# First scale vector of a two-layer encoder kernel: matrix columns moved past one column of silu(c), sums left as a row

## The chip, the cores and the metric

The kernel runs on one core of one Trainium2 chip. The metric is the device time of one execution in microseconds (us). PE is TensorE, DVE is VectorE, ACT is ScalarE, POOL is GpSimd, and SP is SyncE, which here only issues transfers.

## What is computed

A hybrid encoder trunk of two layers on x of 256 rows and 2048 columns. Each sub-layer is preceded by an RMS norm, modulated with a shift and a scale that are projected from the vector c:

```python
def _modulate(x, shift, scale):
    return _rmsnorm(x) * (1 + scale[:, None, :]) + shift[:, None, :]

mod_all = jnp.einsum('bd,lde->lbe', jax.nn.silu(c), ada_w) + ada_b[:, None, :]
for i in range(DEPTH):
    shift1, scale1, gate1, shift2, scale2, gate2 = jnp.split(mod_all[i], 6, axis=-1)
    h = _modulate(x, shift1, scale1)
    ...
    # layer 0: time mixing (three D x D projections of token-shifted h first), layer 1: sparse attention
    x = x + gate1[:, None, :] * y
    h = _modulate(x, shift2, scale2)
    x = x + gate2[:, None, :] * _swiglu(h, f_w1[i], f_w3[i], f_w2[i])
```

`silu(c)` is one vector of 2048, and `ada_w` is 2 x 2048 x 12288. Nothing of the first layer can be projected before its first shift and scale (4096 of the 12288 columns, all 2048 rows: 33.6 MB of float32) are known.

## The kernel before

The stage that the change touches is `Prologue`, the first of the program. It turns x into columns (p.x, 16 tiles of 128 features by 256 tokens), forms the sums of squares, and computes shift 1 and scale 1 of layer 0. `self.sc` holds silu(c) as 128 x 16: row p holds c[16p] to c[16p+15].

The needed part of ada_w is cut into 32 **units** of 1 MB. A unit is (q, piece, kk): q is a quarter of the 2048 outputs (512 of them), piece 0 is the shift and 1 the scale, and kk selects four of the sixteen k, so a unit is 128 x (4 x 512). Unit n lies in quarter n // 8. Even units are shifts (piece 0), odd units are scales (piece 1).

- SP loads the units in order into a ring of six slots (`first_ring`, of which two are named `ada_ring`). Load n waits until unit n-6 has been used (`after_part`). The first four weight units of the following projection (`raw`) go ahead of the last two ring loads, four more behind them.
- DVE takes the even units (`add_part`): four instructions of 128 x 512 each multiply by a column of silu(c) and add into `ada_acc`. What is left is a sum over 128 partitions.
- PE takes the odd units (`part`): per unit 16 products whose stationary operand is a 128 x 128 block of the unit and whose moving operand is one column of silu(c). They accumulate as columns in a PSUM bank, after one product with zeros (L1006) that opens the group. After the quarter's last odd unit PE also sums `ada_acc` over the partitions with four products with a column of ones (L1017), and `ada_summed` is raised.
- `quarter_dve` waits for that, adds the bias into `mod` (L979), and with `quarter_act` applies scale and shift to four tiles of x, mixes them with the previous token and splits them into high and low parts for the first projection. The order on DVE is: the first even unit of the next quarter, `quarter_dve`, the other three even units.

The fourth quarter is finished inside the first projection (`Linear`, L1672 and L1673): PE multiplies with the tiles of quarters 0 to 2, then takes the last odd unit (31), then goes on with the tiles of quarter 3. On DVE the four `split_lo` (L1660) of the projection's first weights stand behind unit 28 and ahead of unit 30. SP, ACT, DVE and PE each run their own program in order, and semaphores join them.

A float32 product shows in the trace as two records on PE, each with a record of its weight load (PEld).

Of the kernel before, what the change touches and what calls it, by code (L numbers as in the profile page):

```python
# [12 lines left out]
P = 128  # L13
# [28 lines left out]
ACT = mybir.ActivationFunctionType  # L42
# [9 lines left out]

LINEAR_ARMED = ("group_taken0", "group_taken1", "hidden", "hid_lo")
HEADS_ARMED = ("logits", "probs", "pturned", "barred_logits", "pT", "vh", "o_lo", "uk_turned", "vhp")
PROLOGUE_ONLY = ("c_loaded", "rows_loaded", "x_loaded", "made", "first_vector", "first_scalar", "first_tensor", "part_added", "first_loaded0", "first_loaded1",
                 "first_loaded2", "first_loaded3", "first_loaded4", "first_loaded5")
BESIDE_MIXING = ("ada_loaded0", "ada_loaded1", "ada_summed", "ada_added", "mod_ready")
ARMED = frozenset(LINEAR_ARMED + HEADS_ARMED)
# [685 lines left out]
class Prologue:  # L744
# [5 lines left out]

    has_pool = True
    slots = 6
    bank = (7, 5, 4, 6)
    units = [(q, piece, kk) for q in range(4) for kk in range(4) for piece in range(2)]
    last = 2
    vector_done = dict(silu=0, tables=1, x_odd=6, one_more=10, normed=14, h_odd=30)
    scalar_done = dict(sigmoid=0, x_even=1, squared=5, h_even=21)
    ident_made, all_made = 9, 38
    tables = [(0, 96, PV_MU), (1, 128, PV_W0), (2, 96, PV_ADA), (3, 96, PV_ADA + 96), (4, 5, PV_KVN)]

    def __init__(self, prog, mixed, first):
# [62 lines left out]
    def pool(self, pool):  # L824
        p, nc, s = self.p, self.p.nc, self.p.s
# [6 lines left out]

        def wait():
            pool.wait_ge(s("made"), count[0])
        for t, v in ((p.ident, 0.0), (p.ones, 1.0), (p.blk, 0.0), (p.zeros, 0.0)):
            made(nc.gpsimd.memset(t[:], v))
        for n, v in enumerate((RMS_EPS, GN_EPS, 8 * 0.6931471805599453, 0.0)):
            made(nc.gpsimd.memset(p.cst[:, n:n + 1], v))
# [19 lines left out]
        q = p.square  # L858
# [46 lines left out]

    def quarter_act(self, act, q):
        p, nc, s, m = self.p, self.p.nc, self.p.s, self.mixed
        self.after_vector(act, "normed", KT)
        act.wait_ge(s("mod_ready"), q + 1)
        for k in (4 * q, 4 * q + 2):  # L910
            nc.scalar.activation(p.hpad[:, k, 1:T + 1], p.hpad[:, k, 1:T + 1], ACT.Identity, scale=p.mod[:, 16 + k:17 + k],
                                 bias=p.mod[:, k:k + 1]).then_inc(s("first_scalar"), 1)
        for k in range(4 * q, 4 * q + 4):
            if k % 2:
                self.after_vector(act, "h_odd", k // 2 + 1)
            else:
                self.after_scalar(act, "h_even", k // 2 + 1)
            m.m1(act, k, k)
            if k > 4 * q:
                m.copy(act, k - 1, (k - 1) % 4)  # L920
        m.copy(act, 4 * q + 3, 3)
# [52 lines left out]
    def quarter_dve(self, dve, q):  # L974
        p, nc, s, m = self.p, self.p.nc, self.p.s, self.mixed
        dve.wait_ge(s("ada_summed"), q + 1)
        for piece in range(2):
            at = 16 * piece + 4 * q
            last = nc.vector.tensor_tensor(p.mod[:, at:at + 4], p.ps[:, self.bank[q], 4 * piece:4 * piece + 4],  # L979
                                           p.pv[:, PV_ADA + at:PV_ADA + at + 4], ADD)  # L980
        last.then_inc(s("mod_ready"), 1)
        if q == 3:
            dve.sem_inc(s("ada_added"), 32)
        self.after_vector(dve, "normed", KT)
        dve.wait_ge(s("mod_ready"), q + 1)
        for k in (4 * q + 1, 4 * q + 3):
            nc.vector.tensor_scalar(p.hpad[:, k, 1:T + 1], p.hpad[:, k, 1:T + 1], p.mod[:, 16 + k:17 + k], p.mod[:, k:k + 1], MUL,
                                    ADD).then_inc(s("first_vector"), 1)
        for k in range(4 * q, 4 * q + 4):
            m.first(dve, k)  # L990
            if k > 4 * q:
                m.low(dve, k - 1)
        m.low(dve, 4 * q + 3)

    def part(self, pe, n):

        p, nc, s = self.p, self.p.nc, self.p.s
        q, piece, kk = self.units[n]
        slot = n % self.slots
        if n % 8 == 1:  # L1000
            self.after_vector(pe, "silu", 1)
            if q == 3:
                pe.wait_ge(s("ln_ms"), 1)
            elif q:
                self.after_vector(pe, "tables", 5)
            nc.tensor.matmul(p.ps[:, self.bank[q], 0:8], p.ones[:], p.zeros[:], start=True, stop=False, skip_group_check=True)  # L1006
        pe.wait_ge(s(f"first_loaded{slot}"), 16 * (n // self.slots + 1))
        for r in range(4):
            for m in range(4):
                last = nc.tensor.matmul(p.ps[:, self.bank[q], 4 * piece + m:4 * piece + m + 1],  # L1010
                                        p.first_ring[slot][:, r * 512 + m * P:r * 512 + (m + 1) * P], p.sc[:, 4 * kk + r:4 * kk + r + 1],
                                        start=False, stop=False, skip_group_check=True)
        last.then_inc(s("first_tensor"), 1)
        if n % 8 == 7:
            self.after_part(pe, n - 1)
            for m in range(4):
                last = nc.tensor.matmul(p.ps[:, self.bank[q], m:m + 1], p.ada_acc[:, q * 512 + m * P:q * 512 + (m + 1) * P], p.ones[:, 0:1],  # L1017
                                        start=False, stop=True, skip_group_check=True)
            last.then_inc(s("ada_summed"), 1)

    def squares(self, pe, ks):
        p, nc, s = self.p, self.p.nc, self.p.s
# [5 lines left out]
    def tensor(self, pe):  # L1028
        p, nc, s, ps = self.p, self.p.nc, self.p.s, self.p.ps
        pe.wait_ge(s("made"), self.ident_made)  # L1030
        pe.wait_ge(s("rows_loaded"), 16 * len(self.rows))
        for n, (t, r, at) in enumerate(self.tables):
            last = nc.tensor.transpose(ps[:, 4 + n // 4, (n % 4) * P:(n % 4) * P + r], p.prow[0:r, t, :], p.ident[0:r, 0:r])
# [12 lines left out]
            last.then_inc(s("first_tensor"), 1)  # L1046
        for n in range(1, len(self.units) - self.last, 2):
            self.part(pe, n)
            if n in (1, 3):
                self.squares(pe, range(8) if n == 1 else range(8, KT))  # L1050
                if n == 3:
                    self.after_square(pe, KT - 1)
                    pe.sem_inc(s("sum_square"), 1)
# [9 lines left out]
    def last_quarter_pe(self, pe):  # L1063
        for n in range(len(self.units) - self.last + 1, len(self.units), 2):
            self.part(pe, n)


class IndexKey:
# [382 lines left out]
class Program:  # L1451
# [25 lines left out]
    def s(self, name):  # L1477

        if name not in self.sems:
            self.sems[name] = self.nc.alloc_semaphore(name)  # L1480
        return self.sems[name]
# [11 lines left out]
    def layout(self):  # L1493
        nc = self.nc
        at = [16512]

        def place(name, shape, dt=F32, offset=None):
            size = 4
            for n in shape[1:]:
                size *= n  # L1500
            if offset is None:
                offset = at[0]
                at[0] += (size + 31) // 32 * 32
            t = nc.alloc_sbuf_tensor_at(name, shape, dt, offset=offset)
            return t, offset
# [27 lines left out]
        self.mod, _ = place("mod", [P, 192])  # L1533
        self.sc, _ = place("sc", [P, KT])
        self.cst, _ = place("cst", [P, 4])
        self.zeros, _ = place("zeros", [P, 8])
        self.rstd, _ = place("rstd", [P, T])
        self.tmp, _ = place("tmp", [P, 2, T])
        assert at[0] <= 229368, at[0]
# [2 lines left out]
        v = lambda name, shape, off, dt=F32: place(name, shape, dt, off)[0]  # L1542
# [983 lines left out]
```

## Time and profile before

| | |
|---|---|
| time, median of 3 runs | 2915.11 us (2911.92 to 2917.52) |
| the profiled execution's own time | 2915.85 us |
| its span | 2914.0 us |
| PE busy | 2763.1 us, 95% of the span |
| DVE busy / ACT busy | 1977.1 us (68%) / 1324.1 us (45%) |
| first product of the first projection (L1672) | at 131.96 us |
| PE resumes with quarter 3's tiles | at 153.04 us |

Times within the profile are counted from the span's start. "Granted clock" (PEclk) is the share of TensorE's 2.4 GHz that the chip let through: 0.50 is its lower level, 1.2 GHz. A PE row's busy time includes time in which records overlap; what one costs in a stream is the distance between starts.

### The profile page before, as it was taken

How to read it: one execution, taken by the hardware profiler on the slowest of the kernel's cores; microseconds unless marked ns; L12 is line 12 of the kernel's file. 1: busy time of each engine (PE TensorE's matmuls, PEld its weight loads, DVE VectorE, ACT ScalarE, POOL GpSimd, SP SyncE). 2: the span in 40 equal slices, each digit the busy share in tenths (PEclk: the TensorE clock that was granted, in tenths of full speed). 3: DMA queues.
4: the chain of work that ended last, by engine and by line, in shares of the span. 5: the costliest groups of instructions: out<-in, count | busy, mean ns of one | idle time of the engine just before them, and what ended most of it. 6: DMA issues, size and time to landing. Idle time of an engine off the chain costs nothing.

```text
span 2914.0 us, 55879 instructions
## 1 busy us (share of the span) xinstructions
PE 2763.1 (95%) x21025; PEld 2423.0 (83%) x21025; DVE 1977.1 (68%) x2611; ACT 1324.1 (45%) x2018; POOL 45.1 (2%) x90
## 2 busy tenths in 40 slices
PE   8999997888988999999999979988989999999998
PEld 7988886788877888888888868877878888888886
DVE  5468852787867777777777786644767755555556
ACT  2155544444444554344444444345445534444444
POOL 1000002000000000000000000000000000000000
PEclk7599999999999999999999989999989999999999
DMA  8869857444447778778788768632848856666653
GB/s 304 277 208 312 300 166 252 136 147 132 144 161 240 256 265 288 273 262 278 261 283 273 246 235 275 216 116 63 279 162 273 291 184 188 185 191 188 186 173 116
DMA packets 484947, 640.02 MB, mean 220 GB/s; under 512 B 21909, under 2 KB 427834, under 8 KB 468154
## 3 DMA queue, kind: packets, MB, share of 16 engines
q1 hardware_dynamic: 480954, 625.31, 64.9%
q0 software_dynamic: 3840, 12.59, 1.2%
q8 instruction: 107, 1.75, 0.3%
q14 instruction: 46, 0.38, 0.0%
HBM read 623.14 MB, written 14.68 MB: 219 GB/s over the span
## 4 chain that ended last, share of the span: by engine, by line
PE 64%; DVE 4%; ACT 2%; issue 1%; DVEq 0%; ACTq 0%
PE ps L1672 40%; PE ps L1673 20%; DVE wlo L1660 1%; PE ps L1719 1%; PE ps L1347 1%; PE ps L1338 1%; DVE ada_acc L1705 1%; ACT whi L1655 1%; DVE nt L133 0%; DVE act L146 0%; PE ps L1374 0%; PE ps L1741 0%; DVE gsum L100 0%; DVE nt L1415 0%; DVE x L319 0%
## 5 line engine op out<-in xcount | busy, mean ns | idle before, releaser
L1672 PE MATMUL ps<-act,whi 128*128 128x512 f32 x3808 | 1359.2, 402 | 27.1 <-DVE act L146 16.3
L1660 DVE TENSOR_TENSOR wlo<-raw,whi 128x1024 fp32r<-128x1024 f32 (+1 forms) x768 | 901.4, 1192 | 499.4 <-ACT whi L1655 496.8
L1655 ACT ACTIVATE whi<-raw 128x1024 fp32r<-128x1024 f32 (+1 forms) x768 | 774.9, 1030 | 667.6 <-PE ps L1673 664.3
L1673 PE MATMUL ps<-act,wlo 128*128 128x256 f32 x3808 | 1073.2, 282 | 0.0
L1672 PEld LDWEIGHTS ps<-act,whi 128*128 128x128 f32 x3808 | 725.5, 191 | 208.9 <-issue 22.5
L1672 PE MATMUL ps<-hid,whi 128*128 128x512 f32 x2176 | 775.6, 398 | 12.2 <-DVE wlo L1660 9.3
L1673 PEld LDWEIGHTS ps<-act,wlo 128*128 128x128 f32 x3808 | 728.2, 191 | 0.0
L1673 PE MATMUL ps<-hid,wlo 128*128 128x256 f32 x2176 | 615.8, 283 | 0.0
L1672 PEld LDWEIGHTS ps<-hid,whi 128*128 128x128 f32 x2176 | 412.8, 190 | 113.5 <-DVE wlo L1660 11.5
L1673 PEld LDWEIGHTS ps<-hid,wlo 128*128 128x128 f32 x2176 | 412.2, 189 | 0.0
L1705 DVE SCALAR_TENSOR_TENSOR ada_acc<-ada_ring,sc,ada_acc 128x2048 f32<-128x2048 f32 x128 | 300.3, 2346 | 0.3
L95 ACT ACTIVATE small<-ps 128x512 f32<-128x512 f32 x176 | 102.2, 581 | 35.4 <-PE ps L1673 35.4
L346 ACT ACTIVATE hid<-hf 128x512 f32 (+1 forms) x44 | 27.8, 632 | 157.8 <-DVE hf L360 157.8
L1847 DVE SCALAR_TENSOR_TENSOR ada_acc<-ada_ring,sc,ada_acc 128x512 f32<-128x512 f32 x120 | 89.6, 747 | 2.4
L311 ACT ACTIVATE tmp<-x 128x512 f32 (+1 forms) x32 | 20.2, 632 | 113.2 <-DVE x L319 113.2
L319 DVE SCALAR_TENSOR_TENSOR x<-gsum,mod,x 128x256 f32 (+1 forms) x128 | 56.4, 482 | 12.4 <-DVE gsum L100 11.6
L1010 PEld LDWEIGHTS ps<-sc,first_ring 128*128 128x128 f32 x320 | 63.9, 310 | 0.6 <-issue 0.5
L1010 PE MATMUL ps<-sc,first_ring 128*128 128x1 f32 x320 | 64.0, 335 | 0.1
L363 DVE TENSOR_TENSOR hid<-hf,hid 128x512 f32 (+1 forms) x44 | 30.5, 693 | 44.3 <-ACT hid L346 44.3
L1900 ACT ACTIVATE DX<-ps 128x512 f32<-128x512 f32 x64 | 37.2, 592 | 49.5 <-PE ps L2233 49.4
L343 ACT ACTIVATE sig<-sgt 128x512 f32<-128x512 f32 x44 | 27.8, 632 | 66.7 <-DVE sgt L100 66.6
L2233 PE MATMUL ps<-DX 64*64 64x64 f32 x1280 | 47.6, 220 | 3.0 <-issue 1.3
(280 smaller groups left out, 2347.3 us busy)
## 6 DMA issues: line engine op xcount, KB each, us to landing
raw<-in_f_w SPq DMA_DIRECT2D x480, 512.0 KB, 4.5
ada_ring<-in_ada_w SPq DMA_DIRECT2D x172, 1024.0 KB, 7.4
raw<-in_a_w_rkv SPq DMA_DIRECT2D x96, 512.0 KB, 5.0
raw<-in_b_w_in SPq DMA_DIRECT2D x56, 512.0 KB, 4.5
raw<-in_f_w SPq DMA_DIRECT2D x64, 384.0 KB, 4.1
first_ring<-in_ada_w SPq DMA_DIRECT2D x20, 1024.0 KB, 7.8
raw<-in_a_w_o SPq DMA_DIRECT2D x32, 512.0 KB, 7.2
raw<-in_b_w_o SPq DMA_DIRECT2D x32, 512.0 KB, 5.5
```

Of the source, the lines that this page charges most:

```text
L95: p.nc.scalar.activation(self.small[:, g], p.ps[:, 2 * g:2 * g + 2, T:2 * T], ACT.Copy).then_inc(p.s(f"small_out{g}"), 1)
L319: last = p.nc.vector.scalar_tensor_tensor(p.x[:, bass.ds(m, 1), :], p.gsum[:, g, b:b + 1, :], p.mod[:, bass.ds(m + 16 * self.gate, 1)], p. ...
L363: nc.vector.tensor_tensor(p.hid_lo[:, bass.ds(i * 2, 2), :], p.hf[:], p.hid_hi[:, bass.ds(i * 2, 2), :].bitcast(F32), SUB).then_inc(s("hid ...
L1010: last = nc.tensor.matmul(p.ps[:, self.bank[q], 4 * piece + m:4 * piece + m + 1], p.first_ring[slot][:, r * 512 + m * P:r * 512 + (m + 1) ...
L1655: self.nc.scalar.activation(self.whi[:, u % SPL, 0:n], self.raw[:, u, 0:n], ACT.Copy).then_inc(self.s("hi_ready"), 1)
L1660: self.nc.vector.tensor_tensor(self.wlo[:, u % SPL, 0:n], self.raw[:, u, 0:n], self.whi[:, u % SPL, 0:n].bitcast(F32), SUB).then_inc(self. ...
L1672: self.nc.tensor.matmul(o, hi[:, kk, c0:c1], src[:, k].rearrange("p a t -> p (a t)"), start=k == 0, stop=False)
L1673: last = self.nc.tensor.matmul(o[:, T:2 * T], lo[:, kk, c0:c1], src[:, k, 0, :], start=False, stop=k == ktotal - 1)
L1705: self.nc.vector.scalar_tensor_tensor(self.ada_acc[:], self.ada_ring[:, j % 2, :], self.sc[:, bass.ds(r * 2 + (a % 16 + j), 1)], self.ada_ ...
L1847: last = nc.vector.scalar_tensor_tensor(acc, row, self.sc[:, n:n + 1], acc, MUL, ADD)
L1900: nc.scalar.activation(dst, src, ACT.Copy, scale=scale).then_inc(s(name), 1)
L2233: last = nc.tensor.matmul(o[h], lhsT[h], rhs[h], start=start, stop=stop, skip_group_check=True)
```

## The change

Four edits, all in `Prologue`:

1. `part`: the operands of the odd units change sides. The stationary operand is one column of silu(c) (128 x 1), the moving operand is 128 x 512 of the unit. Four products for a unit take the place of sixteen, and the sums of a quarter leave as one row of 512 in partition 0 of bank 7 or 5. The product with zeros goes.
2. `row_out` is new, on ACT: it copies that row of 512 from PSUM to SBUF.
3. `sums` is new, on PE: the four products with ones for the shift, as before, and four products of contraction one (row block of 128 as stationary operand, a single 1.0 as moving one) that turn the scale's row into columns. Both go to bank 4.
4. `sums(q)` stands behind the first odd unit of the next quarter; before, the four products with ones stood behind the last odd unit of their own. For quarter 3 it stands behind unit 31.

```diff
-    bank = (7, 5, 4, 6)
+    rows_bank, sums_bank = (7, 5, 7, 5), 4
@@ quarter_act
         p, nc, s, m = self.p, self.p.nc, self.p.s, self.mixed
+        self.row_out(act, q)
         self.after_vector(act, "normed", KT)
@@ part
-        if n % 8 == 1:
-            self.after_vector(pe, "silu", 1)
-            if q == 3:
-                pe.wait_ge(s("ln_ms"), 1)
-            elif q:
-                self.after_vector(pe, "tables", 5)
-            nc.tensor.matmul(p.ps[:, self.bank[q], 0:8], p.ones[:], p.zeros[:], start=True, stop=False, skip_group_check=True)
+        if kk == 0:
+            self.after_vector(pe, "tables", 5)
+            if q >= 2:
+                pe.wait_ge(s("row_out"), q - 1)
         pe.wait_ge(s(f"first_loaded{slot}"), 16 * (n // self.slots + 1))
         for r in range(4):
-            for m in range(4):
-                last = nc.tensor.matmul(p.ps[:, self.bank[q], 4 * piece + m:4 * piece + m + 1],
-                                        p.first_ring[slot][:, r * 512 + m * P:r * 512 + (m + 1) * P], p.sc[:, 4 * kk + r:4 * kk + r + 1],
-                                        start=False, stop=False, skip_group_check=True)
+            last = nc.tensor.matmul(p.ps[0:1, self.rows_bank[q], :], p.sc[:, 4 * kk + r:4 * kk + r + 1],
+                                    p.first_ring[slot][:, r * 512:(r + 1) * 512], start=kk == 0 and r == 0, stop=kk == 3 and r == 3)
         last.then_inc(s("first_tensor"), 1)
-        if n % 8 == 7:
-            self.after_part(pe, n - 1)
-            for m in range(4):
-                last = nc.tensor.matmul(p.ps[:, self.bank[q], m:m + 1], p.ada_acc[:, q * 512 + m * P:q * 512 + (m + 1) * P], p.ones[:, 0:1],
-                                        start=False, stop=True, skip_group_check=True)
-            last.then_inc(s("ada_summed"), 1)
+
+    def row_out(self, act, q):
+
+        p = self.p
+        self.after_part(act, 8 * q + 7)
+        if q:
+            act.wait_ge(p.s("ada_summed"), q)
+        p.nc.scalar.activation(p.stg[1][0:1].rearrange("p a t -> p (a t)"), p.ps[0:1, self.rows_bank[q], :], ACT.Copy).then_inc(p.s("row_out"), 1)
+
+    def sums(self, pe, q):
+
+        p, nc, s = self.p, self.p.nc, self.p.s
+        row = p.stg[1][0:1].rearrange("p a t -> p (a t)")
+        self.after_part(pe, 8 * q + 6)
+        if q:
+            pe.wait_ge(s("mod_ready"), q)
+        for m in range(4):
+            nc.tensor.matmul(p.ps[:, self.sums_bank, m:m + 1], p.ada_acc[:, q * 512 + m * P:q * 512 + (m + 1) * P], p.ones[:, 0:1],
+                             start=True, stop=True)
+        pe.wait_ge(s("row_out"), q + 1)
+        for m in range(4):
+            last = nc.tensor.matmul(p.ps[:, self.sums_bank, 4 + m:5 + m], row[:, m * P:(m + 1) * P], p.ones[0:1, 0:1], start=True, stop=True)
+        last.then_inc(s("ada_summed"), 1)
@@ tensor
             self.part(pe, n)
+            if n % 8 == 1 and n > 1:
+                self.sums(pe, n // 8 - 1)
@@ last_quarter_pe
             self.part(pe, n)
+        self.sums(pe, 3)
```

On PE, from the last odd unit of quarter 0 to the first projection, before (L1010 is a product of a unit with silu(c), L1017 the sum of `ada_acc`, x16 is one unit):

```order
L1010 MATMUL ps<-sc,ada_ring 128x1 x16
L1017 MATMUL ps<-ones,ada_acc 128x1 x4
L1006 MATMUL ps<-zeros,ones 128x8
L1010 MATMUL ps<-sc,first_ring 128x1 x32
L1010 MATMUL ps<-sc,ada_ring 128x1 x16
L1010 MATMUL ps<-sc,first_ring 128x1 x16
L1017 MATMUL ps<-ones,ada_acc 128x1 x4
```

The same place of the changed kernel (L1007 is a product of a unit with silu(c), x4 is one unit; L1027 the sum of `ada_acc`; L1031 the turning of the row, read from the staging tile `stg`):

```order
L1007 MATMUL ps<-ada_ring,sc 1x512 x4
L1007 MATMUL ps<-first_ring,sc 1x512 x4
L1027 MATMUL ps<-ones,ada_acc 128x1 x4
L1031 MATMUL ps<-ones,stg 128x1 x4
L1007 MATMUL ps<-first_ring,sc 1x512 x4
L1007 MATMUL ps<-ada_ring,sc 1x512 x4
L1007 MATMUL ps<-first_ring,sc 1x512 x8
L1027 MATMUL ps<-ones,ada_acc 128x1 x4
```

Behind each quarter's last odd unit one unit of the next quarter (4 products) now comes before the sums, and four more small products follow them.

On ACT, from the norm to the first tiles of quarter 0 in the changed kernel (`stg<-ps 1x512` is `row_out`; L912 applies scale and shift, L174 mixes):

```order
L1762 ACTIVATE rstd<-ps,cst 128x256
L1764 ACTIVATE rstd<-rstd 128x256
L1017 ACTIVATE stg<-ps 1x512
L912 ACTIVATE hpad<-hpad,mod 128x256 x2
L174 ACTIVATE m_89<-hpad,omu 128x256 x2
```

Only the row with `stg` is new there. It stands once ahead of each of the four quarters' work, the fourth time behind the four `split_hi` of the first projection. The programs of DVE and SP keep their order.

## Rows read from the trace of the kernel before

**Rows 1.** Windows: busy time of each engine, PEclk, DMA share, GB/s
```profile
core 0: us, PE busy (x) PEld busy (x) DVE busy (x) ACT busy (x) POOL busy (x), PEclk, DMA share, GB/s
35.00:40.00 5.00, 5.00 (x14) 2.82 (x13) 0.00 (x0) 2.48 (x6) 0.00 (x0) 0.64 1.05 387
45.00:50.00 5.00, 5.00 (x27) 5.00 (x27) 4.89 (x12) 0.00 (x0) 0.00 (x0) 0.54 0.64 211
...
60.00:80.00 20.00, 20.00 (x95) 20.00 (x95) 10.05 (x14) 0.00 (x0) 0.00 (x0) 0.50 0.90 316
80.00:100.00 20.00, 20.00 (x96) 20.00 (x95) 14.53 (x27) 4.16 (x10) 0.00 (x0) 0.50 0.77 262
...
135.00:140.00 5.00, 5.00 (x23) 4.27 (x22) 0.00 (x0) 0.00 (x0) 0.00 (x0) 0.74 0.51 163
...
150.00:155.00 5.00, 1.96 (x6) 1.67 (x7) 4.20 (x9) 4.68 (x9) 0.00 (x0) 0.50 0.00 0
...
200.00:300.00 100.00, 100.00 (x568) 86.95 (x567) 82.40 (x91) 54.51 (x81) 6.54 (x9) 1.00 0.89 301
...
600.00:620.00 20.00, 18.87 (x474) 17.04 (x474) 18.34 (x44) 10.23 (x27) 0.00 (x0) 1.00 0.49 160
```

**Rows 2.** Timeline of PE: start, duration, instruction, idle before it
```profile
40.91 3.70 PE L1010 MATMUL ps<-sc,first_ring 128*128 128x1 f32 x32
44.48 6.10 PE L1010 MATMUL ps<-sc,ada_ring 128*128 128x1 f32 x32
...
79.91 1.84 PE L1017 MATMUL ps<-ones,ada_acc 128*128 128x1 f32 x8
...
95.69 13.79 PE L1010 MATMUL ps<-sc,first_ring 128*128 128x1 f32 x64
109.35 1.84 PE L1017 MATMUL ps<-ones,ada_acc 128*128 128x1 f32 x8
111.05 0.57 PE L1006 MATMUL ps<-zeros,ones 128*128 128x8 f32 x2
...
131.96 0.77 PE L1672 MATMUL ps<-act,whi 128*128 128x512 f32 x1
...
142.95 3.63 PE L1010 MATMUL ps<-sc,ada_ring 128*128 128x1 f32 x32
146.44 1.03 PE L1017 MATMUL ps<-ones,ada_acc 128*128 128x1 f32 x8
153.04 0.80 PE L1672 MATMUL ps<-act,whi 128*128 128x512 f32 x1 [5.57 <-DVE act L203]
```

**Rows 3.** Timeline of DVE, the same columns
```profile
47.29 3.10 DVE L972 SCALAR_TENSOR_TENSOR ada_acc<-ada_ring,sc,ada_acc 128x512 f32<-128x512 f32 x4
53.07 0.22 DVE L979 TENSOR_TENSOR mod<-ps,pv 128x4 f32<-128x4 f32 x2
58.32 3.11 DVE L972 SCALAR_TENSOR_TENSOR ada_acc<-first_ring,sc,ada_acc 128x512 f32<-128x512 f32 x4
81.79 0.23 DVE L979 TENSOR_TENSOR mod<-ps,pv 128x4 f32<-128x4 f32 x2 [11.17 <-PE ps L1017]
111.23 0.23 DVE L979 TENSOR_TENSOR mod<-ps,pv 128x4 f32<-128x4 f32 x2 [9.80 <-PE ps L1017]
122.87 4.62 DVE L1660 TENSOR_TENSOR wlo<-raw,whi 128x1024 fp32r<-128x1024 f32 x4
147.51 0.23 DVE L979 TENSOR_TENSOR mod<-ps,pv 128x4 f32<-128x4 f32 x2 [16.99 <-PE ps L1017]
```

**Rows 4.** Timeline of SP's issues of ring loads
```profile
50.42 0.92 SPq L819 DMA_DIRECT2D ada_ring<-in_ada_w  x2
73.66 15.74 SPq L819 DMA_DIRECT2D first_ring<-in_ada_w  x4
```

**Rows 5.** The line that issues the ring loads
```profile
DMA to landing us min/median/max: 4.9/8.3/14.3
```

**Rows 6.** Groups of PE, ACT and chain pieces: float32 products elsewhere; a copy of 512
```profile
L1741 PE MATMUL ps<-sqacc,ones 128*128 128x256 f32 x16 | 6.7, 557 | 20.2 <-DVE sqacc L326 20.2
1953.68 3.73 PE ps L1338 x16
L893 ACT ACTIVATE x<-ps 128x512 f32<-128x512 f32 x4 | 2.4, 598 | 13.8 <-PE ps L1044 13.8
```

More of the change, by code:

```diff
@@ L54 @@
 HEADS_ARMED = ("logits", "probs", "pturned", "barred_logits", "pT", "vh", "o_lo", "uk_turned", "vhp")
-PROLOGUE_ONLY = ("c_loaded", "rows_loaded", "x_loaded", "made", "first_vector", "first_scalar", "first_tensor", "part_added", "first_loaded0", "first_loaded1",
+PROLOGUE_ONLY = ("c_loaded", "rows_loaded", "x_loaded", "made", "first_vector", "first_scalar", "first_tensor", "part_added", "row_out", "first_loaded0", "first_loaded1",
                  "first_loaded2", "first_loaded3", "first_loaded4", "first_loaded5")
@@ L757 @@
     scalar_done = dict(sigmoid=0, x_even=1, squared=5, h_even=21)
-    ident_made, all_made = 9, 38
+    ident_made, all_made = 8, 37
     tables = [(0, 96, PV_MU), (1, 128, PV_W0), (2, 96, PV_ADA), (3, 96, PV_ADA + 96), (4, 5, PV_KVN)]
@@ L834, in wait @@
             pool.wait_ge(s("made"), count[0])
-        for t, v in ((p.ident, 0.0), (p.ones, 1.0), (p.blk, 0.0), (p.zeros, 0.0)):
+        for t, v in ((p.ident, 0.0), (p.ones, 1.0), (p.blk, 0.0)):
             made(nc.gpsimd.memset(t[:], v))
@@ L978, in quarter_dve @@
             at = 16 * piece + 4 * q
-            last = nc.vector.tensor_tensor(p.mod[:, at:at + 4], p.ps[:, self.bank[q], 4 * piece:4 * piece + 4],
+            last = nc.vector.tensor_tensor(p.mod[:, at:at + 4], p.ps[:, self.sums_bank, 4 * piece:4 * piece + 4],
                                            p.pv[:, PV_ADA + at:PV_ADA + at + 4], ADD)
@@ L1535, in layout @@
         self.cst, _ = place("cst", [P, 4])
-        self.zeros, _ = place("zeros", [P, 8])
         self.rstd, _ = place("rstd", [P, T])
```

## The prediction

> **What bounds the kernel now.** I read the windows first, then the timelines of PE, DVE and SP. From 200 us on PE is busy without a gap at the full clock [rows 1], so whatever time the first stage gives or takes moves the rest of the program as a block. The question is only when PE gets to the first projection's quarter 3, which is at 153.04 us [rows 2].
>
> In the stage itself PE is the bound as well, but not by its arithmetic. From 60 to 100 us it is busy in all 40 us at a granted clock of 0.50, 1.2 GHz, while DVE works 24.6 of them and the transfers run at 316 and 262 GB/s where the chip gave 387 from 35 to 40 us [rows 1]. Two odd units take 13.79 us in that stretch, 6.9 each; at the full clock one takes 3.70 us [rows 2]. DVE waits 11.17 and 9.80 us for PE's sums of quarters 1 and 2 [rows 3], and SP's four ring loads from 73.66 us spread over 15.74 us because their slots are PE's [rows 4]. Quarters follow each other at 29.4 us (81.79 to 111.23, rows 3): four units of 6.9, the 1.84 of the sums, less some overlap, and a bit for the product with zeros (0.57).
>
> So PE loads 128 x 128 weights to move one column, and while it does so its clock stays at the lower level. The stream of 128x512 products from 131.96 us [rows 2] brings it back: 0.74 on average from 135 to 140 us [rows 1].
>
> **The odd unit.** 32 records with one moving column become 8 with 512. The trace has no product with one stationary column. The nearest float32 row is L1338: 16 records of 256 columns in 3.73 us at the full clock, 233 ns each [rows 6]. A record of 512 costs at most twice that, so 8 cost at most 3.73 us; the weight load in it, now a single column, is what may fall off. I take 3.5 at the full clock and 6.9 at half, twice that less what doesn't scale. So at an equal clock **the unit costs what it did** (3.70 and 6.9). Everything hangs on whether the clock rises.
>
> What the rows say: after streams of 256 and 512 moving columns it has risen or stayed up (0.74 from 135 us, 1.00 from 200 us), and it is at 1.00 from 600 to 620 us, where the program has 64x64 products with 64 moving columns, a part of the array [rows 1]. In the one-column stream it fell (0.54 from 45 to 50 us, then 0.50) though PE's weight load was busy all along [rows 1]. On their moving side the new products are like the streams that run fast. Against it: none of these rows has fewer than 64 stationary columns, and the new products do exactly the multiplications that the old ones did at 0.50. I take the first likeness, at 7 in 10.
>
> The Trainium skill ("TensorE: Matmul & The Clock Gate", Part 1, What's actually happening) says that the throttled state is the default and that the chip sets the clock by how busy the PE has been recently. By that sentence alone the old stream, busy in all 40 us of two windows, should have run at 1.00, its units at 3.7 us each, and the change would be worth nothing; the trace disagrees, at 0.50.
>
> **With the full clock, step by step.** The start is not PE's. The slot of unit 6 comes free when DVE has added it, at 50.4 us (47.29 + 3.10, rows 3), and load 12 is issued at 50.42 [rows 4]; that DVE work hangs on the norm, which the change leaves. PE has units 5, 7 and now 9 to do from 40.91 [rows 2]: 3 x 3.5 gives 51.4. Then `sums(0)`. Its first half cost 1.03 us at the full clock [rows 2], and the second half, four products with 128-column weight loads and one row, I price the same; between nothing and 1.84 (the half-clock row). So 53.4 us, where DVE's mod came at 53.07 before: no change, and the extra unit ahead of the sums is paid by units 5 and 7 being faster (unit 7 took from 44.48 to 50.58 before, rows 2).
>
> From there one loop sets the pace:
> - DVE's work of the quarter: 5.3 (53.07 to 58.32, rows 3), with the wake-up;
> - its next addition, which frees a ring slot: 3.15 (3.11, rows 3);
> - the transfer into it: 0.45 to issue (0.92 for two, rows 4) and 4.9 to land at the least [rows 5], 5.4;
> - the transfer behind it, the next quarter's first odd unit: 2.7 (1.049 MB at 387 GB/s, rows 1);
> - that unit on PE, 3.5, and the sums, 2.0.
>
> Sum 22.1 us for a quarter, where it was 29.4. The transfers alone ask 8 x 2.71 = 21.7, so ring and memory bind together, and PE (4 x 3.5 + 2.0 = 16.0) and DVE (4 x 3.15 + 5.3 = 17.9) do not. So the sums of quarters 1 and 2 are ready at 75.6 and 97.7 instead of 81.7 and 111.2.
>
> After `sums(2)` DVE has its quarter (5.3), units 26 and 28 (6.3) and the first weight split (4.62 / 4 = 1.16, rows 3): 110.5 us. PE's odd units 27 and 29 are done at about 106.5, the first weights have landed at about 104. So the first projection starts at **110.5 us, not 131.96**; DVE now sets that, and PE has stood 4 us and starts cold as before. Its three first blocks took 11.0 us (131.96 to 142.95, rows 2) and do so again: 121.5. Unit 31 has landed by then (20 loads and 2.1 MB of weights from 50.4: 50.4 + 0.45 + 2.2 + 22 x 2.71 = 112.7, and about 1 for the loop), so it costs 3.5. Then the products with ones 1.0, under which lies the new copy on ACT (0.6 by L893's 598 ns for 128 partitions [rows 6]; its floor is nothing); the turning 1.0; handovers 0.2. That is 5.7 where unit and sums took 4.56 (142.95 to 147.51, rows 2 and 3), and the one place where the new work is bare: 1.0 us lost. From mod to the next product 5.53 us (147.51 to 153.04, rows 2 and 3) stays: **132.7 us**.
>
> Gain 153.04 - 132.7 = 20.3 us. From the profiled execution's 2915.85 that gives 2895.5; it is 0.7 above the median, so 2895 for a median.
>
> The zero product that goes (0.57 each) and the opening waits (`tables` is long done) are worth nothing on a PE that waits. Three things could shift the number: the projection starting at the full clock (its 11.0 would be near 8.3, an estimate by the gap between the clock's two levels over the first 5 us: 2.6 more gain); transfers at 350 GB/s instead of 387, as where weights and units mix (some 2 to 5 less); the second half of the sums at its ends (a loop passes it three times and the tail once: 4 less, or at 1.84 each 3 more).
>
> **The rivals.**
> - *The clock swings (0.12).* In the loop PE waits about 1.9 us for each second transfer and 4 us before the projection, and a gap has brought the lower clock in the rows: 0.50 from 150 to 155 us, behind 5.57 us of waiting [rows 1, 2]. The skill's same page (HAM oscillation) warns of just this: bursts of products between waits for transfers fall back to the lower level every time. Against a lasting effect: at half the clock a unit (6.9) is longer than its pair of transfers (5.4), so the waits vanish and the stream is solid, as from 131.96. With 5.0 us for a unit on average and 1.4 for each half of the sums, PE's quarter is 22.8 and the loop 24.4; two loops, the parts before and behind, and the tail give some 143 us: gain 10, **2906**. The range of this case is 2901 to 2911.
> - *The clock stays at half (0.14): slower.* Units stay 6.9, nothing comes sooner, and the new work is bare. PE's quarter is 4 x 6.9 + 2 x 1.84 = 31.3 against 29.4, twice 1.9. `sums(0)` behind unit 9 comes at about 62 (three units from 40.9, of which two ran faster before), some 2 us late against what PE had done by then before. PE reaches the projection at 138.3, 6.3 late, and the tail adds the 1.0: 7 us, **2923** (2917 to 2927). It is decided by PE's quarter: above 29.4 + 1.9 the loss passes 0.2%, and that is where the second half of the sums costs what the first does.
> - *The products are dearer than their columns (0.04): slower.* L1741's records of 256 columns last 557 ns on average where few stand in a row [rows 6]. If 512 columns with a change of weights ahead of each took twice that, a unit would cost 8.9 us; PE's quarter 39.3, 10 more over three and the tail: some 30 us, **2946**. Against it: L1338's 233 ns in a stream.
>
> **How the numbers follow.** Forecast 0.70, its own range 2888 to 2903 by the three shifts. A measurement here tells 0.2%, about 5.8 us, from no change. Faster: 0.70 and nearly all of the swinging clock, 0.80. Within 0.2%: the rest of that and part of the half clock, 0.06. Slower: 0.14. A range for 8 in 10 has the forecast and the swinging clock: 2887 to 2912.
>
> **What would show it.** In the profile after: L1007 at about 440 ns a record and a PEclk of 1.00 from 50 to 105 us, DMA near 380 GB/s there; DVE's mod rows at about 53, 76 and 98 us and idle time before them that ends with a transfer's landing rather than PE's backlog; the projection's first product at 110 and its second part at 133. PEclk at 0.50 in those windows, records of 850 ns and a full PE would show the prediction wrong at the clock; a clock of 1.00 with less gain, wrong at the loop.

## The result and the profile after

The changed kernel takes **2894.48 us** (median of 10 runs, 2886.68 to 2906.56) where the one before takes 2916.32 (10 runs, 2905.68 to 2922.15): a ratio of 0.9928, 95% interval 0.9911 to 0.9946. The forecast was 2895. The profiled execution's own time is 2888.72 us, its span 2887.1.

The first stage, in windows of 5 and 20 us (the columns are those of [rows 1]):

```profile
45.00:50.00 5.00, 5.00 (x25) 2.41 (x23) 4.49 (x10) 0.05 (x1) 0.00 (x0) 1.00 0.75 254
...
65.00:70.00 5.00, 3.76 (x5) 0.60 (x6) 2.10 (x3) 0.00 (x0) 0.00 (x0) 0.67 1.05 388
...
80.00:85.00 5.00, 3.23 (x9) 0.57 (x8) 4.72 (x7) 0.00 (x0) 0.00 (x0) 1.00 0.56 192
...
60.00:80.00 20.00, 17.36 (x48) 4.49 (x48) 12.03 (x24) 4.75 (x11) 0.00 (x0) 0.91 1.05 389
80.00:100.00 20.00, 14.20 (x41) 3.90 (x40) 12.41 (x21) 2.77 (x6) 0.00 (x0) 0.91 0.93 340
```

Where PE was busy without a gap at 0.50 and the transfers ran at 316 and 262 GB/s [rows 1], PE now works 31.6 of 40 us at 0.91, and the transfers run at 389 and 340.

The timeline of PE in the changed kernel (L1007 is a unit's products, L1027 the sums of `ada_acc`, L1031 the turning of the row, L1687 the first projection):

```profile
40.59 3.60 PE L1007 MATMUL ps<-ada_ring,sc 128*1 128x512 f32 x8
...
47.55 1.05 PE L1027 MATMUL ps<-ones,ada_acc 128*128 128x1 f32 x8
48.54 1.05 PE L1031 MATMUL ps<-ones,stg 1*128 1x1 f32 x8
...
60.34 3.59 PE L1007 MATMUL ps<-first_ring,sc 128*1 128x512 f32 x8 [1.78 <-DMA first_ring<-in_ada_w]
66.24 5.29 PE L1007 MATMUL ps<-first_ring,sc 128*1 128x512 f32 x8 [2.30 <-DMA first_ring<-in_ada_w]
...
89.98 5.29 PE L1007 MATMUL ps<-ada_ring,sc 128*1 128x512 f32 x8 [4.03 <-DMA ada_ring<-in_ada_w]
95.20 1.05 PE L1027 MATMUL ps<-ones,ada_acc 128*128 128x1 f32 x8
...
110.22 0.47 PE L1687 MATMUL ps<-act,whi 128*128 128x512 f32 x1 [4.53 <-issue]
...
120.28 3.59 PE L1007 MATMUL ps<-ada_ring,sc 128*1 128x512 f32 x8
...
131.40 0.79 PE L1687 MATMUL ps<-act,whi 128*128 128x512 f32 x1 [5.57 <-DVE act L203]
```

A unit costs 3.6 us, as one did at the full clock before [rows 2], and PE now waits for transfers, not they for it. PE resumes with quarter 3 at 131.40 us where it was 153.04 [rows 2]: **21.6 us sooner**. The medians differ by 21.8.

DVE, the mod of quarters 0 to 3 (to be read beside [rows 3]), and the addition that frees a slot after quarter 1:

```profile
49.62 0.23 DVE L980 TENSOR_TENSOR mod<-ps,pv 128x4 f32<-128x4 f32 x2 [0.22 <-PE ps L1031]
...
54.88 3.11 DVE L973 SCALAR_TENSOR_TENSOR ada_acc<-first_ring,sc,ada_acc 128x512 f32<-128x512 f32 x4
...
73.53 0.23 DVE L980 TENSOR_TENSOR mod<-ps,pv 128x4 f32<-128x4 f32 x2 [6.35 <-PE ps L1031]
...
78.93 3.11 DVE L973 SCALAR_TENSOR_TENSOR ada_acc<-ada_ring,sc,ada_acc 128x512 f32<-128x512 f32 x4
...
97.27 0.23 DVE L980 TENSOR_TENSOR mod<-ps,pv 128x4 f32<-128x4 f32 x2 [6.04 <-PE ps L1031]
...
125.87 0.23 DVE L980 TENSOR_TENSOR mod<-ps,pv 128x4 f32<-128x4 f32 x2 [9.32 <-PE ps L1031]
```

The first three mod rows are 23.9 and 23.7 us apart; they were 28.7 and 29.4. The slot that the addition at 78.93 frees is loaded again at once (timeline of SP):

```profile
82.06 0.92 SPq L819 DMA_DIRECT2D ada_ring<-in_ada_w  x2
```

**How the runs are compared.** Of the span, what lies behind the resumption is 2761.0 us in the trace before (2914.0 - 153.04) and 2755.7 in the one after. Over the 14 traces of this study, one for each kernel, it lies between 2746 and 2775, with no tie that I see to what was changed ahead of it. So a single time of a kernel tells little here, and most experiments are read at one place: **the time at which PE resumes with quarter 3's tiles** (the L1672 row with 5.57 us of waiting for DVE before it; its line number shifts with the edit). That place isn't free of scatter either: PE's first unit begins anywhere from 20.1 to 21.4 us in these traces, so differences of under 1 us at the resumption say nothing.

### The profile page after: what moved, and what is told of

The parts are those of the page before. It is cut to its first block, busy times and chain, and to the rows that moved or that the text cites. A ratio compares the mean times of both kernels' runs of the same rounds, so it can differ in the third digit from the quotient of the medians.

```text
span 2887.1 us, 55171 instructions
## 1 busy us (share of the span) xinstructions
PE 2715.8 (94%) x20665; PEld 2333.5 (81%) x20665; DVE 1977.4 (68%) x2611; ACT 1326.1 (46%) x2022; POOL 45.0 (2%) x89
## 4 chain that ended last, share of the span: by engine, by line
PE 64%; DVE 5%; ACT 2%; issue 2%; DVEq 0%; ACTq 0%
PE ps L1687 40%; PE ps L1688 20%; DVE wlo L1675 1%; PE ps L1734 1%; PE ps L1363 1%; PE ps L1354 1%; DVE ada_acc L1720 1%; DVE nt L133 1%; ACT whi L1670 1%; DVE act L146 1%; PE ps L1390 0%; PE ps L1756 0%; DVE gsum L100 0%; DVE nt L1431 0%; DVE x L319 0%
## 5 line engine op out<-in xcount | busy, mean ns | idle before, releaser
L1687 PE MATMUL ps<-act,whi 128*128 128x512 f32 x3808 | 1349.7, 399 | 32.8 <-DVE act L146 17.7
L1687 PEld LDWEIGHTS ps<-act,whi 128*128 128x128 f32 x3808 | 723.7, 190 | 208.8 <-issue 27.6
L1687 PE MATMUL ps<-hid,whi 128*128 128x512 f32 x2176 | 775.4, 399 | 12.3 <-DVE wlo L1675 9.3
L1687 PEld LDWEIGHTS ps<-hid,whi 128*128 128x128 f32 x2176 | 413.4, 190 | 113.0 <-DVE wlo L1675 11.6
L1915 ACT ACTIVATE DX<-ps 128x512 f32<-128x512 f32 x64 | 37.1, 592 | 53.5 <-PE ps L2248 53.4
L2248 PEld LDWEIGHTS ps<-DX 64*64 64x64 f32 x1280 | 45.3, 143 | 5.7 <-issue 5.7
L100 DVE TENSOR_TENSOR gsum<-ps,small 128x512 f32<-128x512 f32 x64 | 43.7, 683 | 7.4 <-ACT small L95 7.4
```

The costliest lines, as they stand in the source:

```text
L100: p.nc.vector.tensor_tensor(out, p.ps[:, 2 * g:2 * g + 2, 0:T], self.small[:, g], ADD).then_inc(p.s(f"group_taken{g}"), 1)
L1687: self.nc.tensor.matmul(o, hi[:, kk, c0:c1], src[:, k].rearrange("p a t -> p (a t)"), start=k == 0, stop=False)
L1915: nc.scalar.activation(dst, src, ACT.Copy, scale=scale).then_inc(s(name), 1)
L2248: last = nc.tensor.matmul(o[h], lhsT[h], rhs[h], start=start, stop=stop, skip_group_check=True)
```

## The experiments

**1. One wide product beside each old unit.** Is it the sides of the operands, or would the old ones gain as much with a clock that is kept up? The kernel before, with:

```diff
             self.part(pe, n)
+            if n >= 5:
+                self.fill(pe, 1)     # ones times 512 columns of x into bank 0, result unread
```

> The kernel before, operands as they were, with one extra product behind each odd unit from unit 5 to 29 whose result nobody reads (ones times 512 columns of x, into a free bank). Theory (the gain came from the clock, not from the operands' sides): PEclk 1.00 from 45 us on, the 16 one-column products of a unit take 3.7 us instead of 6.9, the extra product 0.9, so a unit is 4.6, under the 5.4 of its pair of transfers; PE resumes with quarter 3's tiles at 124 to 131 us instead of 153, and the time falls by 20 us or more. Rival (the clock stays down, the gain was in the swapped sides): a unit takes 6.9 and the extra product 0.9 to 1.7, PE resumes at 165 to 175 us, and the time rises by 12 to 22 us.

Measured: 2940.87 us, ratio 1.009 (1.0064 to 1.0117), resumption at 177.47 us, 2.5 past the rival's bound. Window and timeline of PE (L1024 is the added product):

```profile
60.00:80.00 20.00, 20.00 (x83) 17.93 (x83) 13.47 (x21) 1.22 (x4) 0.00 (x0) 0.50 0.65 228
...
65.39 2.06 PE L1024 MATMUL ps<-x,ones 128*128 128x512 f32 x2
67.24 6.83 PE L1010 MATMUL ps<-sc,first_ring 128*128 128x1 f32 x32
```

The clock stayed at 0.50, and a unit with its added product took 8.5 us from start to start, where a unit alone took 6.8. The theory fell in the form in which I had put it: one wide product behind a unit doesn't bring the clock back.

**2 and 3. Two and three wide products within each old unit.** The same product, behind the first and third group of four one-column products (r in (0, 2)), or behind the first three (r < 3).

> The kernel before with two products of 512 columns of x (result unread) among the 16 one-column products of each odd unit from 5 to 29; one such product behind the unit had left the clock at 0.50. Theory (what the change gains is the clock that its stream keeps, and old operands would gain too if theirs were kept): should the clock come back, PEclk is 1.00, a unit takes 3.65 + 1.72 = 5.4 us, and PE resumes at about 137 us although it does 1.5 times the work. Rival (no such filling brings it back): 0.50, 6.8 + 3.7 = 10.5 us a unit, and PE resumes at 200 us or later.

> As the run with two, with three wide products in each odd unit. If the clock comes back here and not with two, a unit takes 3.65 + 2.6 = 6.2 us, PE is the bound with 26 us for a quarter, and it resumes at 142 to 148 us, still ahead of the 153.0 of the kernel before, with nearly double its work. If not: 12.4 us a unit, and 220 us or later.

Measured, one run each: resumption at 196.53 and 209.65 us, 2964.86 and 2976.41 us beside 2913.07 for the kernel before. The windows of the one with three:

```profile
40.00:50.00 10.00, 9.85 (x61) 7.48 (x60) 7.96 (x20) 0.92 (x3) 0.00 (x0) 1.00 0.53 188
50.00:60.00 10.00, 10.00 (x51) 7.26 (x50) 7.66 (x18) 4.13 (x10) 0.00 (x0) 0.79 1.00 359
60.00:80.00 20.00, 20.00 (x67) 15.31 (x66) 11.30 (x16) 0.00 (x0) 0.00 (x0) 0.50 0.41 138
```

With three the fall came later than without them (1.00 in the window to 50 us, where the kernel before had 0.54 from 45 to 50 [rows 1]), but it came, and from 60 us the clock was 0.50. Each added product then costs 1.7 us. The rivals' side was right, but both resumptions came ahead of its bounds of 200 and 220 us, by 3.5 and 10.4. No kernel with the old operands was brought to a lasting full clock, so that one would be as fast as the changed one is argued (3.63 us for unit 31 at the full clock, rows 2) and not shown.

**4. New sides, old width.** The changed kernel, each product cut into four of 128 moving columns:

```diff
-            last = nc.tensor.matmul(p.ps[0:1, self.rows_bank[q], :], p.sc[:, 4 * kk + r:4 * kk + r + 1],
-                                    p.first_ring[slot][:, r * 512:(r + 1) * 512], start=kk == 0 and r == 0, stop=kk == 3 and r == 3)
+            first = kk == 0 and r == 0
+            for m in range(1 if first else 4):
+                at = slice(0, 512) if first else slice(m * P, (m + 1) * P)
+                last = nc.tensor.matmul(p.ps[0:1, self.rows_bank[q], at], p.sc[:, 4 * kk + r:4 * kk + r + 1],
+                                        p.first_ring[slot][:, r * 512 + at.start:r * 512 + at.stop], start=first,
+                                        stop=kk == 3 and r == 3, skip_group_check=True)
```

> The changed kernel with each product of 512 moving columns cut into four of 128 (a quarter's very first stays whole): one stationary column as in the change, 16 products and 16 weight loads a unit as before. Theory (the swapped sides carry the clock, the width only saves instructions): PEclk stays at 1.00 outside waits, records follow each other every 107 to 130 ns, a unit takes 3.5 to 4.2 us, PE resumes within 3 us of 131.4. Rival (it is the 512 columns at a stretch that keep the clock): 0.50, 6.9 us a unit, resumption at 155 to 165.

Measured: resumption at 129.70 us (2906.39 us in its one run, 2913.07 for the kernel before). A window and PE's timeline:

```profile
60.00:80.00 20.00, 14.05 (x117) 10.15 (x118) 13.97 (x26) 4.75 (x11) 0.00 (x0) 1.00 1.03 376
...
78.86 3.65 PE L1010 MATMUL ps<-first_ring,sc 128*1 128x128 f32 x32 [1.78 <-DMA first_ring<-in_ada_w]
```

As many products and weight loads as the old unit, 32 records each, the same multiplications, and yet 3.65 us at 1.00 instead of 6.9 at 0.50. It is the change of sides that carries the clock, not the fewer instructions, and products of 512 are worth next to nothing beyond products of 128 here (3.59 against 3.65 us a unit). PE has waits in this stream that the old one doesn't have; experiment 5 shows the new sides at 1.00 without any. Which of the two sides does it, the narrow stationary operand or the wide moving one, isn't separated by any run.

**5. The new units twice.** Does a unit of the old price take the whole gain away? The changed kernel, with each product of units 5 to 29 done a second time into a free bank (the calls are shortened here):

```diff
+            if 5 <= n < 31:
+                nc.tensor.matmul(p.ps[0:1, 0, :], ..., start=True, stop=True)
             last = nc.tensor.matmul(p.ps[0:1, self.rows_bank[q], :], ...)
```

> The changed kernel with the products of odd units 5 to 29 done twice, the second set into a free bank, so that at the full clock a unit costs 6.9 us, what the old one did at half. Theory (what was gained is the unit's price alone): PE is the bound again, a quarter takes 29.6 us, and PE resumes at 151 to 156 us where it was 153.0 before: the gain is gone. Rival (part of the gain has another source, such as the norm that comes sooner or the new place of the sums): it resumes at 148 or sooner.

Measured, one run: PE resumes at 152.94 us.

```profile
60.00:80.00 20.00, 20.00 (x50) 4.12 (x50) 15.81 (x28) 4.13 (x10) 0.00 (x0) 1.00 0.65 237
```

```profile
117.35 1.05 PE L1030 MATMUL ps<-ones,ada_acc 128*128 128x1 f32 x8
...
141.81 3.59 PE L1010 MATMUL ps<-ada_ring,sc 128*1 128x512 f32 x8
...
152.94 0.79 PE L1690 MATMUL ps<-act,whi 128*128 128x512 f32 x1 [5.57 <-DVE act L203]
```

That is 0.1 us from the kernel before, and within what was expected. The price of a unit is the gain. That it fits to 0.1 us is luck: the projection starts 1.2 us later than before (133.13 against 131.96), its three blocks, all at the full clock, take 8.7 instead of 11.0, and the tail has its 1.0 of new work. (Its time was 2903.31, 12 us below the earlier kernel's span for span at the same resumption: the part behind it took 2748.7 us, one of the short ones.)

**6. The old sums moved.** The kernel before with edit 4 alone: the four products with ones in a function of their own, called behind the next quarter's first odd unit, for quarter 3 behind unit 31.

> The kernel before with one part of the change alone: the products with ones stand behind the next quarter's first odd unit. PE is busy throughout there, so nothing is lost on PE: mod of quarters 0 to 2 comes 7 us later each, PE resumes at 152 to 154 us as before, and the time is the same. Rival (DVE's later quarter holds a ring slot long enough to make PE wait): 2 us or more later.

Measured, one run: mod of quarters 0 to 2 at 59.06, 88.50 and 117.94 us, 6 to 7 later than in [rows 3], and resumption at 152.47. As expected at that place: where PE is the bound throughout, the place of the sums costs nothing. Its one time, 2928.42 us, is 10.6 above the 2917.86 of the kernel before; 2773.6 of its span lie behind the resumption, one of the long ones.

**7. The sums at the end of their own quarter.** With PE no longer the bound, does that place now cost?

```diff
             self.part(pe, n)
-            if n % 8 == 1 and n > 1:
-                self.sums(pe, n // 8 - 1)
+            if n % 8 == 7:
+                self.sums(pe, n // 8)
```

> The changed kernel with the sums of quarters 0 to 2 behind the last odd unit of their own quarter, not behind the next quarter's first. PE then waits bare for the copy on ACT (0.7 us). Theory (a loop through the next quarter's first odd unit, its transfer and DVE's slot sets the pace): the sums of quarters 1 and 2 no longer wait for a transfer that itself waited for DVE; the loop breaks, the transfers run at 387 GB/s without the dip at 80 to 85 us, the first projection starts at 101 to 104 us instead of 110.2 and PE resumes at 122 to 125 instead of 131.4; time 6 to 9 us below the changed kernel. Rival (the memory's rate alone sets it): start and resumption within 1 us of the changed kernel's.

Measured: **2887.86 us**, ratio 0.99 (0.9876 to 0.9924), projection from 105.17 (1.2 us past the range), resumption at 124.79 us (within it). From 80 to 85 us the transfers ran at 387 GB/s, where the changed kernel had 192.

**8. Two units ahead on DVE.** The other end of the same loop:

```diff
             self.add_part(dve, 8 * q + 8)
+            self.add_part(dve, 8 * q + 10)
             self.quarter_dve(dve, q)
-            for n in range(8 * q + 10, min(8 * q + 16, len(self.units) - self.last), 2):
+            for n in range(8 * q + 12, min(8 * q + 16, len(self.units) - self.last), 2):
```

> The changed kernel with the sums where it has them, and DVE adding two units of the next quarter ahead of each quarter's work, not one. Theory of the loop: slot 8q+10 comes free some 7 us earlier, so load 8q+16 does, and the loop breaks at its other end; the quarter's work on DVE begins 0 to 2 us later for it. Start of the projection at 101 to 105 us, resumption at 122 to 126. Rival (memory's rate alone): as the changed kernel, 110 and 131. Rival (DVE's order is what counts, its quarter work must come first): later than 131.

Measured: **2886.56 us**, ratio 0.9906 (0.9882 to 0.993), projection from 103.35, resumption at 122.97 us. DVE and PE:

```profile
68.85 3.11 DVE L974 SCALAR_TENSOR_TENSOR ada_acc<-ada_ring,sc,ada_acc 128x512 f32<-128x512 f32 x4 [1.90 <-DMA ada_ring<-in_ada_w]
71.88 0.22 DVE L981 TENSOR_TENSOR mod<-ps,pv 128x4 f32<-128x4 f32 x2
...
93.56 0.22 DVE L981 TENSOR_TENSOR mod<-ps,pv 128x4 f32<-128x4 f32 x2
```

```profile
87.95 3.59 PE L1008 MATMUL ps<-ada_ring,sc 128*1 128x512 f32 x8 [1.93 <-DMA ada_ring<-in_ada_w]
...
122.97 0.80 PE L1688 MATMUL ps<-act,whi 128*128 128x512 f32 x1 [5.57 <-DVE act L203]
```

Quarter 2 now follows quarter 1 at 21.7 us, the eight transfers' own time; PE's waits for a transfer are 2.50 us at the most, and no unit from 45 us on takes 5.3.

**9. Both.** The edits of 7 and 8 together.

> The edits of the two kernels before it together. Theory: either one already leaves the transfers as the only bound, so both give no more than the better one, within 1.5 us at the resumption (122 to 125 us). Rival (each removes a wait of its own): 3 us or more below the better one.

Measured: ratio 0.9896 (0.9866 to 0.9927), resumption at 123.60 us (one of its six runs took 7759.88 us, for which I have no explanation, and is left out of the comparison; the median of the other five is 2889.95). Nothing more than the better one, as the theory of one loop with two ends has it.

**10. PE's waits filled.** The changed kernel with unread products where PE waited:

```diff
             if n % 8 == 1 and n > 1:
                 self.sums(pe, n // 8 - 1)
+            if n in (15, 23, 29):
+                self.fill(pe, {15: 2, 23: 4, 29: 4}[n])
```

> The changed kernel with products whose result nobody reads (ones times 512 columns of x, 0.87 us each) put where PE waited in its trace: 2 behind unit 15, 4 behind unit 23, 4 behind unit 29. Theory (the clock falls in a wait, and units 17 and 25 then cost 5.3 instead of 3.6 on the way that sets the pace): both units take 3.6, mod of quarter 1 comes 1.7 us sooner and of quarter 2 about 3, the first projection starts 3 us sooner at about 107 and its three blocks take 8.5 to 9 instead of 10.1; PE resumes at 126 to 128 instead of 131.4. Rival (the clock of those two units costs nothing, a transfer ends last anyway): resumption within 1 us of 131.4, or later by the added products.

Measured, one run: resumption at 127.56 us, 3.8 us sooner for 9 us of useless work on PE (2874.77 us, the part behind a short one, 2745.6).

```profile
63.62 1.99 PE L1037 MATMUL ps<-x,ones 128*128 128x512 f32 x4
65.94 3.59 PE L1007 MATMUL ps<-first_ring,sc 128*1 128x512 f32 x8 [0.34 <-DMA first_ring<-in_ada_w]
...
89.24 3.59 PE L1007 MATMUL ps<-ada_ring,sc 128*1 128x512 f32 x8
...
107.79 0.47 PE L1694 MATMUL ps<-act,whi 128*128 128x512 f32 x1 [0.35 <-issue]
...
116.43 3.59 PE L1007 MATMUL ps<-ada_ring,sc 128*1 128x512 f32 x8
```

Units 17 and 25 cost 3.6 instead of 5.3, and the projection's three blocks 8.6 (107.79 to 116.43) instead of 10.1. Mod of quarter 1 came at 71.53 (73.53 without), 1.7 us of it by unit 17 and 0.3 by an earlier landing. Mod of quarter 2 came at 94.83 (97.27), 2.4 sooner, where a loop that carries the 2.0 on and adds unit 25's 1.7 would give 3.7: the four added products themselves held unit 25 up. Load 24 was issued at 80.07 instead of 82.06, 7.9 us from issue to unit as in the changed kernel would give 88.0 (an estimate), and PE was busy with the added products from 85.61 to 89.24.

**11. The turning four times.** `for m in [0, 1, 2, 3] * 4` in `sums`.

> The changed kernel with the four one-row products of each sums done four times (3 x 0.98 = 2.9 us more each). Theory (the sums lie on the loop in every quarter and bare in the tail): mod later by 2.9 for quarter 0, 5 to 6 for 1, 8 to 9 for 2, and PE resumes 10 to 12 us later, at 142 to 143. Rival (in the loop they are covered, only the tail is bare): 3 us later, 134 to 135. By the same rows one pass of the turning is worth 1 us at the resumption or nearly 4.

Measured, one run: mod at 52.49, 78.88, 107.07 and 139.41 us, 2.9, 5.4, 9.8 and 13.5 later than in the changed kernel, resumption at 144.94, 13.5 later. The sums are on the loop in every quarter. The delay is 1.5 us past the upper end of what was expected, and more than four times 2.9: the clock was down in parts of the turning itself, which took 3.92 us in quarter 0 but 5.54 in quarter 2 and 4.68 in the tail. Two units that had no wait before them, and took 3.6 in the changed kernel, took 5.04 and 5.29 right behind the turning. So this run gives no clean price for one pass; it shows where the sums lie, and that every pass counts.

**12. The best of them, and unit 6 earlier.** Experiment 8 with DVE's addition of unit 6 ahead of the wait for the norm:

```diff
-        for n in range(0, 6, 2):
+        for n in range(0, 8, 2):
             self.add_part(dve, n)
         self.after_scalar(dve, "x_even", 4)
         dve.wait_ge(s("rstd"), 1)
         ...
-        for n in range(6, 8, 2):
-            self.add_part(dve, n)
```

> The run with two units ahead (resumption at 122.97 us), and DVE adds unit 6 before it waits for the norm, not behind the 16 products with it. In the earlier runs DVE stood idle 6.5 us there, and load 12 was issued at 46.7 us for want of unit 6's slot, with the transfers at 254 GB/s from 45 to 50 us. Theory (the transfers are the only bound left): load 12 goes out at 41 to 42 us, no dip is left, every later landing is 2 to 3 us sooner and PE resumes at 120 to 121.5 us; time 10 to 13 us below the changed kernel, 1.1% below the one before. Rival (the slots of units 8 and 10 bind next): 122.5 to 123.

Measured: **2885.45 us**, ratio 0.9897 (0.987 to 0.9923), resumption at 122.06 us.

```profile
45.00:50.00 5.00, 5.00 (x24) 2.39 (x22) 4.72 (x7) 0.31 (x1) 0.00 (x0) 1.00 1.05 385
50.00:60.00 10.00, 7.47 (x18) 1.26 (x18) 8.62 (x19) 4.14 (x10) 0.00 (x0) 1.00 1.05 387
60.00:80.00 20.00, 15.99 (x48) 4.22 (x46) 14.97 (x28) 4.75 (x11) 0.00 (x0) 1.00 1.05 387
```

Load 12 went out at 41.70 and the dip is gone, as expected, but the resumption is only 0.9 us sooner than in 8, not 2 to 3, between the ranges of theory and rival. The time is 9.0 us below the changed kernel's, not 10 to 13. The dip in 8, 5 us at 238 instead of 387 GB/s, is worth 1.9 us at the most, and this run's first unit began 0.4 us later (21.03 against 20.62). I had counted the issue's advance, not the idle time of the transfers. By the times, 7, 8, 9 and 12 can't be told from each other; all lie below the changed kernel's 0.9928, with intervals that overlap it at the edge. By the resumption all four stand clear of the changed kernel (124.79, 123.60, 122.97 and 122.06 against 131.40); among 8, 9 and 12 the neighbours lie within the scatter.

## Why the prediction was right

**PE was the bound through its clock.** Right, and shown from two sides: at an equal number of records and multiplications the new sides run at 1.00 (experiment 4), and when the unit is given its old price the gain is gone (5). The price of a unit was forecast as 3.5 and is 3.43 from start to start (40.59 to 44.03 for unit 7, 3.6 with its end). The likeness by which I chose the full clock, at 7 in 10, was weaker than I wrote: in the 0.64 from 35 to 40 us of [rows 1] PE was doing products of 256 moving columns, between one-column units. That it was the right likeness is what the runs show, not what the rows did.

**The start is not PE's, 53.4 us for the first sums.** This step failed: `sums(0)` was ready at 49.5. I had taken the norm as untouched. Its 16 products of 256 columns stand between PE's units 1, 3 and 5. Before and after:

```profile
23.93 5.99 PE L1025 MATMUL ps<-tmp,ones 128*128 128x256 f32 x16
```

```profile
24.06 4.75 PE L1038 MATMUL ps<-tmp,ones 128*128 128x256 f32 x16
```

Between one-column units they ran at a granted clock of 0.66 (25 to 30 us) and took some 6 us for each eight; between the new units they take 4.75 at 1.00, and unit 3 takes 3.5 instead of 4.8. PE reached unit 5 at 37.16 and not 40.91, and DVE, which waits for the norm, had added unit 6 by 46.6 and not 50.4. That is 3.9 us of gain that the forecast lacked; the start was PE's after all.

**The loop of 22.1 us.** The mechanism was right, a term mis-sized. Measured from the rows above for quarter 1 to 2: quarter's work 5.4 (73.53 to 78.93), addition 3.1, issue and both transfers 7.9 (82.06 to 89.98; forecast 8.1), the unit 5.2 (forecast 3.5), sums 2.1: 23.7. The unit is dearer because PE had waited 4.03 us for it and the clock had gone down: the swinging clock that was a rival at 0.12 is there, once in each quarter. It doesn't decide, since it costs 1.7 us a quarter, once, where the rival had every unit dearer (5.0 on average), a loop of 24.4 for 22.1 and 10 us in all. Filled waits (10) give part of it back, with 1.5 more in the projection. The Trainium skill ("TensorE: Matmul & The Clock Gate", HAM oscillation) describes this pattern: where a burst of products is shorter than the wait for its next transfer, each burst starts at the lower clock. The trace agrees for the unit behind 4.03 us of waiting (5.29 us); of the waits shorter than a unit, 1.78 us left the clock up (3.59) and 2.30 us did not (5.29). That the loop runs through DVE's slot and the next quarter's unit is shown by 7 and 8, which cut it at either end and give 6.6 and 8.4 us at the resumption, and by 9, which gives no more.

**Transfers and ring bind together.** Too generous: in the changed kernel the transfers idle for want of slots (192 GB/s from 80 to 85 us, 254 from 45 to 50). Alone they would give what 8 and 12 show from quarter 1 to 2, 21.7 us.

**Projection at 110.5, then 11.0, 5.7 and 5.5.** Measured 110.22, 10.1, 5.6 (120.28 to 125.87), 5.5. The blocks are 0.9 us faster: the projection's first products still ran at the full clock (0.47 us for the one at 110.22, 0.77 for the one at 131.96 before [rows 2]), where the forecast had a cold start. Bare new work in the tail is 1.0 us, as forecast: 5.59 where it was 4.56.

The terms off: 3.9 sooner at the start, two loops 1.7 later each, projection 0.3 earlier in its start by these and 0.9 in its blocks; 131.40 instead of 132.7. Two errors of opposite sign nearly cancel, 3.9 against 3.4: the mechanism was foreseen, that the time is met within 1 us is luck.

**The rivals.** *The clock stays at half* would have needed the likeness of multiplications to hold; the changed kernel's own 1.00 and experiment 4's exclude it for these shapes. No run prices it. Experiment 5 has units of 6.9 but its sums and blocks at the full clock; with three quarters' sums at half (3.7 instead of 2.0) and the blocks at 11.0, an estimate from its 152.94 is 160, the 7 us of loss that I gave. *Dearer than their columns*: records follow each other at 429 ns in the units (3.43 / 8), under the 466 that L1338's row allowed.

**The rest of the program.** That it moves as a block holds for the medians (21.8 against 21.6), not for single runs: the part behind the resumption ranges over 29 us in these traces. Where in it the differences arise isn't settled.

## What to carry to other kernels

For a long stream of float32 matrix-vector products on TensorE, try the vector as the stationary operand, one column, and the matrix as the moving one. At the full clock both orders cost the same here (3.6 us a unit), but the old one ran at 0.50 and the new one at 1.00. An engine that is busy in every microsecond can still be at half its clock, so look at the granted clock before the busy time. When such an engine ceases to be the bound, look at once for the loop that now is (here slot, transfer, unit, sums, and back), because orders that were free before it, as the place of the sums (experiments 6 and 7), cost then. And a wait may cost twice: once itself, and again in the clock of what follows (1.7 us behind the waits of 2.30 and 4.03).

## What was not expected of the hardware

- The clock went down behind waits of 2.30 and 4.03 us in the changed kernel (a unit in 5.29 us) but not behind one of 2.50 in experiment 8 (`60.74 3.60`). The same unit behind nearly the same wait came out both ways in experiments 7 and 9, so a wait's length alone doesn't tell it:

```profile
95.85 5.17 PE L1007 MATMUL ps<-first_ring,sc 128*1 128x512 f32 x8 [3.27 <-DMA first_ring<-in_ada_w]
```

```profile
94.60 3.59 PE L1008 MATMUL ps<-first_ring,sc 128*1 128x512 f32 x8 [3.28 <-DMA first_ring<-in_ada_w]
```

- Wide products in a one-column stream, up to three for sixteen, didn't hold off the fall to 0.50; in experiment 11, 3.9 us of one-column products without a wait were followed by a unit in 5.04 us.
- Turning a row into columns by products with contraction one costs what sums over 128 partitions do: 0.97 us for four products (48.54 to 49.51), 0.24 each, where the four with 128 rows took 0.99 (47.55 to 48.54).
- The copy of a row on a single partition took 586 ns on ACT (L1017), that of 128 partitions 598 [rows 6].
